# First feed-forward block: the down product by the seven-product scheme, the memory rows as a weight panel

## The reference, cut to what matters

```python
def swiglu(h, w_gate, w_up, w_down):              # 1024 -> 2816 -> 1024
    return (silu(h @ w_gate) * (h @ w_up)) @ w_down

shift1, scale1, gate1, shift2, scale2, gate2 = split(c_act @ ada_w[l] + ada_b[l], 6)
x = x + gate2[:, None, :] * swiglu(h, ...)        # layer 0
hk = modulate(rms_norm(x, kv_norm_g), k_shift, k_scale)   # then kv_a = hk @ w_kv_a
h  = modulate(rms_norm(x, norm1_g[1]), shift1, scale1)
mem_n = rms_norm_2(mem, mem_norm[l])              # memory rows, 256 x 1024
```

## Time and profile before

| | |
|---|---|
| median of 3 runs | 1117.94 us |
| profiled execution, its own time | 1117.15 us |
| its span | 1115.3 us |
| PE busy | 1052.3 us (94%) |
| DVE busy | 608.1 us (55%) |
| ACT busy | 294.0 us (26%) |
| DMA, mean over the span | 176 GB/s |

### The profile page before, as it was taken

The page is one execution under the profiler, slowest core; times in us unless marked ns, Lnnn a source line. Parts: engine busy times, 40 slices in busy tenths (PEclk is TensorE's granted clock), DMA queues, the critical chain, the costliest instruction groups (busy, mean ns, idle before and its releaser), DMA issues.

```text
span 1115.3 us, 21577 instructions
## 1 busy us (share of the span) xinstructions
PE 1052.3 (94%) x9373; PEld 909.2 (82%) x9373; DVE 608.1 (55%) x1180; ACT 294.0 (26%) x709; POOL 64.2 (6%) x84
## 2 busy tenths in 40 slices
PE   6879999999999999889999999999997799999997
PEld 4647888888888867678999999988887688898786
DVE  8996445444321727726766575334814561676632
ACT  6512510000000645623001000123323251202641
POOL 3010010110100100000000000000003100000000
PEclk9999999999999999999999999999998999999999
DMA  9995979999845334173654553443440003554220
GB/s 289 367 307 182 301 274 362 344 336 360 326 184 189 106 115 151 37 226 109 188 158 152 163 189 103 144 141 126 132 152 5 4 4 114 189 154 149 76 77 38
DMA packets 128744, 195.81 MB, mean 176 GB/s; under 512 B 4176, under 2 KB 114394, under 8 KB 122250
## 3 DMA queue, kind: packets, MB, share of 16 engines
q1 hardware_dynamic: 118218, 131.15, 37.0%
q0 software_dynamic: 10144, 62.92, 14.9%
q10 hardware_dynamic: 288, 0.36, 0.1%
HBM read 191.53 MB, written 1.05 MB: 173 GB/s over the span
## 4 chain that ended last, share of the span: by engine, by line
PE 82%; DVE 12%; ACT 3%; issue 2%; DMA 0%; SPq 0%; DVEq 0%; ACTq 0%
PE psum L761 45%; PE psum L1147 11%; PE psum L1233 7%; PE psum L1201 6%; DVE arena L1984 4%; PE psum L1774 3%; PE psum L1036 2%; PE psum L1739 1%; ACT arena L3085 1%; DVE sq L1984 1%; DVE arena L2154 1%; DVE arena L1990 1%; PE psum L1714 1%; DVE arena L2248 1%; ACT sq L3085 1%
## 5 line engine op out<-in xcount | busy, mean ns | idle before, releaser
L3085 ACT ACTIVATE arena<-psum 128x256 f32<-128x256 f32 (+6 forms) x229 | 100.6, 466 | 567.3 <-PE psum L761 341.7
L761 PE MATMUL psum<-hT,ring 128*128 128x256 f32 x944 | 211.6, 381 | 2.6 <-DVE hT L1990 1.4
L761 PEld LDWEIGHTS psum<-hT,ring 128*128 128x128 f32 x944 | 177.0, 190 | 30.0 <-issue 7.1
L761 PE MATMUL psum<-arena 64*64 64x64 f32 (+6 forms) x2252 | 91.4, 252 | 16.7 <-issue 11.4
L1984 DVE TENSOR_TENSOR arena<-arena 128x512 f32<-128x512 f32 (+8 forms) x145 | 97.5, 696 | 11.4 <-PE psum L1201 8.6
L761 PE MATMUL psum<-hT,arena 128*128 128x256 f32 (+2 forms) x664 | 94.7, 320 | 4.9 <-DVE hT L1984 4.9
L761 PEld LDWEIGHTS psum<-arena 64*64 64x64 f32 (+3 forms) x2252 | 71.8, 150 | 30.4 <-issue 26.9
L761 PEld LDWEIGHTS psum<-hT,arena 128*128 128x128 f32 (+2 forms) x664 | 82.6, 176 | 16.5 <-issue 6.7
L1984 DVE TENSOR_TENSOR arena<-psum,arena 128x128 f32<-128x128 f32 (+1 forms) x116 | 38.6, 353 | 74.3 <-PE psum L1147 41.1
L1984 DVE TENSOR_TENSOR arena<-arena,psum 128x512 f32<-128x512 f32 (+2 forms) x56 | 30.6, 570 | 72.8 <-ACT arena L3085 41.2
L1990 DVE SCALAR_TENSOR_TENSOR acc<-aring,c_act,acc 128x2048 f32<-128x2048 f32 (+1 forms) x21 | 41.9, 1994 | 37.9 <-DMA aring<-in_kv_ada_w 23.3
(11 more groups left out here) (322 smaller groups left out, 1568.4 us busy)
## 6 DMA issues: line engine op xcount, KB each, us to landing
aring<-in_ada_w POOLq DMA_DIRECT2D x36, 1024.0 KB, 8.4
ring<-in_a_w_in SPq DMA_DIRECT2D x14, 1024.0 KB, 5.4
arena<-in_ffn_w_gate SPq DMA_DIRECT2D x12, 1024.0 KB, 5.5
arena<-in_ffn_w_up SPq DMA_DIRECT2D x12, 1024.0 KB, 8.3
ring<-in_ffn_w_down SPq DMA_DIRECT2D x11, 1024.0 KB, 6.8
ring<-in_ffn_w_gate SPq DMA_DIRECT2D x10, 1024.0 KB, 8.7
ring<-in_ffn_w_up SPq DMA_DIRECT2D x10, 1024.0 KB, 9.5
ring<-in_ada_w POOLq DMA_DIRECT2D x8, 1024.0 KB, 14.4
```

The costliest lines, as they stand in the source:

```text
L761: return eng.matmul(dst, w, x, start=first, stop=last)
L3085: return eng.activation(dst, x, f, **k)
```

## The change

The hidden products of layer 0 stay as they are, chunk by chunk, but the down product now comes behind all of them and goes by the seven-product scheme, in the code that layer 1 uses. FAST names for each layer the j whose gate and up products are halved: none in layer 0. Further: the two sums of down panels 0 and 1 are made at j = 9; the ada panels are dealt out anew (22 of the 36 late ones up to j = 10, the other 14 between the steps of the down product); row blocks 3 to 6 move to later places; block 7 is summed between the two halves of kv_a; the sum of block 6 moves from sq to acc; the memory rows become an entry of the weight list (ring slot 0) behind the twelve down panels, and their transpose moves out of aring.

```diff
-        HALVED = (1,)
+        HALVED = (0, 1)
+        FAST = {0: (), 1: tuple(range(1, NDN))}
...
         swiglu_weights(0)
+        weights.append((a["mem_2"][0].rearrange("(b p) d -> p b d", p=P), (2, D), ("memT", 3)))
...
@@ TensorE
+            def whole_chunks(l, j, g, u):
+                for m in range(2):
+                    c = 2 * j + m
+                    eng.wait_ge(*next_bank(("gu", l, c)))
+                    ...
...
                     for q in range(DOWN_PANELS):
+                        beside_down(i, q)
...
-            def ada_beside(j):
-                if j in (2, 4, 6, 8):
-                    ada_rows(2 + j // 2)
-                if j in (3, 5, 7, 9):
-                    row_columns(2 + j // 2, row_late, "a")
-            swiglu(0, 0, ada_beside)
-            eng.wait_ge(done("mem_landed"), 16)
+            ROWS_AT, COLUMNS_AT = {3: 3, 7: 4, 9: 5}, {4: 3, 8: 4, 10: 5}
+            def ada_beside(j):
+                if j in ROWS_AT:
+                    ada_rows(ROWS_AT[j])
+                if j in COLUMNS_AT:
+                    row_columns(COLUMNS_AT[j], row_late, "a")
+            def ada_beside_down(i, q):
+                if (i, q) == (2, 0):
+                    ada_rows(6)
+                if (i, q) == (2, 2):
+                    row_columns(6, row_late, "a")
+            swiglu_of_halves(0, 0, ada_beside, ada_beside_down)
+            mem_nat, landed = panel()
+            eng.wait_ge(*landed)
...
-            ada_rows(7, "b")
             for b in range(2):
...
+                if b:
+                    ada_rows(7, "b")
@@ VectorE
                     if k == 0:
                         if blk > 4:
-                            eng.wait_ge(*filled_at(("row", blk - 2)))
+                            eng.wait_ge(*filled_at(("row", 3 if blk == 5 else blk - 1)))
...
+                    if j not in fast:
+                        for m in range(2):
+                            c = 2 * j + m
+                            combine_to(j + 1, m + 1)
+                            eng.wait_ge(*filled_at(("gu", l, c)))
+                            eng.wait_ge(done("silu_ready"), silus(l, c))
+                            tt(hid[:, c, :], hid[:, c, :], bank_of(("gu", l, c))[:, T:2 * T], ALU.mult)\
+                                .then_inc(*v.empties(("gu", l, c)))
+                            hid_done[0] = v.last
+                            beside(j, 1)
+                        combine_to(j + 1, 3)
+                        beside(j, 1)
+                        if j % 2 == 0 and j < NDN - 1:
+                            combine_hidden(l, [j - 2, j - 1])
+                        beside(j, 0)
+                        if j == NDN - 2:
+                            combine_down(l, 0)
+                            combine_down(l, 1)
+                        continue
...
-                combine_hidden(l, [NDN - 1])
+                combine_hidden(l, [8, 9, 10])
...
-                combine_down(l, 2)
-                combine_down(l, 3)
-                ahead = 4
+                ahead = 2
                 for i in range(KC // 2):
                     for d in range(ahead, min(3 * i + 6, DOWN_PANELS * KC // 2)):
                         combine_down(l, d)
+                        beside_down(i, d)
                     ahead = 3 * i + 6
+                    beside_down(i, None)
                     down_outputs(i)
...
-            def ada_beside(c):
-                for _ in range(2 if c < 14 else 1):
+            PANELS_BY = [2, 4, 6, 9, 11, 13, 16, 18, 20, 20, 22]
+            def ada_beside(j, n):
+                for _ in range(n):
+                    if ada_next[0] < EARLY + PANELS_BY[j]:
+                        ada_panel()
+                if n == 0 and j in (6, 10):
+                    ada_bias({6: 3, 10: 4}[j])
+            def ada_beside_down(i, d):
+                if d is not None:
                     ada_panel()
-                if c in (7, 11, 15, 19):
-                    ada_bias({7: 3, 11: 4, 15: 5, 19: 6}[c])
-            swiglu(0, ada_beside)
+                else:
+                    for _ in range((0, 0, 1, 3)[i]):
+                        ada_panel()
+                    if i in (1, 3):
+                        ada_bias(5 if i == 1 else 6)
+            swiglu_of_halves(0, 0, lambda i: None, ada_beside, ada_beside_down)
@@ ScalarE: the rows and columns are taken to match, and each block's first product is copied
+            def beside_down(pair):
+                if pair == 2:
+                    take_row(6, row_late)
+                if pair == 3:
+                    take_columns(6)
+                copy_down(0, pair)
+            squares(1, beside_down)
@@ GpSimd
-            eng.wait_ge(done("ada_used"), len(ada_source) - EARLY)
-            eng.dma_start(mem_nat, a["mem_2"][0].rearrange("(b p) d -> p b d", p=P)).then_inc(done("mem_landed"), 16)
```

More of the change, by code:

```diff
@@ L1133, in first_chunks, with swiglu_of_halves @@
                 last.then_inc(*fills(("gu", l, 1)))
-            def swiglu_of_halves(l, h_base):
+            def whole_chunks(l, j, g, u):
+                for m in range(2):
+                    c = 2 * j + m
+                    eng.wait_ge(*next_bank(("gu", l, c)))
+                    ps = bank_of(("gu", l, c)).rearrange("p (m t) -> p m t", t=T)
+                    for i, w in enumerate((g, u)):
+                        for k in range(KC):
+                            last = mm(ps[:, i, :], w[:, k, m * P:(m + 1) * P], hT3[:, k, :], k == 0, k == KC - 1)
+                    last.then_inc(*fills(("gu", l, c)))
+            def swiglu_of_halves(l, h_base, beside=lambda j: None, beside_down=lambda i, q: None):
                 g, landed = panel()
@@ L1217, in swiglu_of_halves @@
                         last.then_inc(*(fills(dn) if q == DOWN_PANELS - 1 else pe.signals("down_panel")))
[L1219 to L1249, removed]
-                        eng.wait_ge(*next_bank(("gu", l, c)))
-                        ps = bank_of(("gu", l, c)).rearrange("p (m t) -> p m t", t=T)
-                        for i, w in enumerate((g, u)):
-                            for k in range(KC):
-                                last = mm(ps[:, i, :], w[:, k, m * P:(m + 1) * P], hT3[:, k, :], k == 0, k == KC - 1)
-                        last.then_inc(*fills(("gu", l, c)))
-                    extra(j)
-                    if j:
-                        down(j - 1)
-                down(NDN - 1)
             def attend(at, steps):
@@ L2315, in combine_weights @@
                 g, u = slot(at), slot(at + 1)
-                s1, s2, s4 = [unit_sums(j)[:, x] for x in range(3)]
+                s1, s2, s4 = [unit_sums(l, j)[:, x] for x in range(3)]
                 if part == 1:
@@ L2382, in first_chunks, with swiglu_of_halves, combine_to @@
                 eng.wait_ge(*filled_at(("gu", l, 1)))
-                eng.wait_ge(done("silu_ready"), silu_base(l) + 2)
+                eng.wait_ge(done("silu_ready"), silus(l, 1))
                 tt(hid[:, 1, :], hid[:, 1, :], bank_of(("gu", l, 1))[:, T:2 * T], ALU.mult)\
                     .then_inc(*v.empties(("gu", l, 1)))
-            def swiglu_of_halves(l, h_base, behind):
+            def swiglu_of_halves(l, h_base, behind, beside=lambda j, n: None, beside_down=lambda i, d: None):
+                fast = FAST[l]
+                parts = [(j, part) for j in fast for part in range(1, 5)]
+                sent = [0]
+                def combine_to(j, part):
+                    while sent[0] < len(parts) and parts[sent[0]] <= (j, part):
+                        combine_weights(l, *parts[sent[0]])
+                        sent[0] += 1
@@ L2414, in swiglu_of_halves @@
                     two_ready = v.last
-                    if j < NDN - 1:
-                        combine_weights(l, j + 1, 3)
-                    else:
+                    if ahead:
+                        combine_to(j + 1, 3)
+                    if l and j == NDN - 1:
                         combine_down(l, 0)
@@ L2424, in swiglu_of_halves @@
                     tt(up[:, :, half_1], ps(p5), u3, ALU.add).then_inc(*v.signals("halves_read"))
-                    if j < NDN - 1:
-                        combine_weights(l, j + 1, 4)
-                    else:
+                    if ahead:
+                        combine_to(j + 1, 4)
+                    if l and j == NDN - 1:
                         combine_down(l, 1)
-                    if j % 2 == 0:
+                    beside(j, 1)
+                    if j % 2 == 0 and j < NDN - 1:
                         combine_hidden(l, [j - 2, j - 1])
@@ L3300, in swiglu_of_halves @@
                 for j in range(1, NDN):
+                    if j not in FAST[l]:
+                        for c in (2 * j, 2 * j + 1):
+                            eng.wait_ge(*filled_at(("gu", l, c)))
+                            act(hid[:, c, :], bank_of(("gu", l, c))[:, 0:T], ACT.Silu).then_inc(*s.signals("silu_ready"))
+                        beside(j)
```

(1 more changed line is left out.)

144 lines of the change are left out of this document (75 added, 69 removed).

## The result

The changed kernel's runs have a median of 1124.55 us (7 runs, 1122.7 to 1127.63) against 1119.52 us for the kernel before beside them (7 runs): ratio 1.0053, 95% interval 1.0039 to 1.0068. A second series gave 1.0039 (1.0026 to 1.0053). It is slower, by 4 to 6 us; "no change" was the forecast, and the time lies above its range. The profiled execution took 1123.88 us, its span 1122.1 us; PE was busy 1049.5 us (94%), DVE 649.8 us (58%), that is 42 us more than before.

The account below looks back on a forecast made before the run. The prediction took TensorE to bound the block. Its terms, -7.17 + 2.2 + 0.9 + 3.8 + 1.0 = +0.7 us on the profiled 1117.15, gave 1117.9, or 1118.7 us as median of runs; range 1112.5 to 1123.5.

Parts of the forecast that it names:

- products: Layer 0's down product: 308 products of 128 columns in 68.79 us in place of 75.96; -7.17 us.
- S: Down product, at the rows of block 6: PE waits for DVE to finish ada panel 28; +2.2 us.
- longer tail of the scheme: Behind the down product: x complete 1.9 us after PE's end, 1.07 before; +0.9 us.
- L: Tail: x late because DVE's last outputs stand behind ada panels waiting for loads; +3.8 us, 1.6 to 7.8 by load time.
- rows 7 between kv_a's halves: Row sums of block 7, moved from a gap ahead of kv_a onto the path between its halves; +1.0 us.
- clock from x to C: Slower TensorE clock from x complete to the second projection: nothing in the sum, priced only in rival (2).
- rival (2): The tail's idle lowers TensorE's clock into kv_a, from about 4 us idle; +2.3 us more, 1121.0 us; chance 0.17.
- upstream at nothing: Panels ahead of the down product, gate and up products, memory rows and weight loads: no added cost, 0 us.
- The aside that 6.15 us a load would give L = 3.2: Tail estimate using the Trainium skill's 6.15 us per 1 MB load for every load; not used in the sum.
- Rival (1): DVE delivers in time, so neither S nor L arises; -5.3 us, 1112.6 us; chance 0.25.
- Rival (3): Loads land in 8 us and more throughout, giving S = 4 and L = 8; +6.7 us, 1124.6 us; chance 0.13.

Follow-up runs that it names:

- e1_warm: The changed kernel with ten constant 128x256 products in PE's tail wait, ahead of the last squares' sums; 1116.25 us, ratio 0.9983 to the kernel before.
- m_late7: m_early with the rows of block 7 summed between kv_a's halves, not ahead of kv_a; 1113.67 us, ratio 0.9951.
- e2_no_last_three: The changed kernel with the last three late ada panels (34 to 36, block 7) neither loaded nor summed; 1120.45 us, ratio 1.0013.
- m_early: The changed kernel with 28 late panels by j = 10, rows 6 at (0, 2), rows 7 ahead of kv_a, no panel before last outputs; 1111.91 us, ratio 0.9938.
- before_late7: The kernel before the change, with only the rows of block 7 moved between kv_a's halves; 1119.49 us, ratio 1.0013.
- e3_rows_later: The changed kernel with the row sum of block 6 one down panel later, at (2, 1) not (2, 0); 1124.53 us, ratio 1.0055.
- e2_rows7_ahead: The changed kernel without the last three late ada panels and with the rows of block 7 summed ahead of kv_a; 1118.02 us, ratio 0.9990.
- e2_warm: e2_no_last_three with six constant 128x256 products ahead of the last squares' sums; 1115.55 us, ratio 0.9974.
- m_warm: m_early with six constant 128x256 products ahead of the last squares' sums; 1111.36 us, ratio 0.9932.

## Why the prediction was wrong

Its terms against what the traces measured, in us from F to C:

| term | predicted | after | second series |
|---|---|---|---|
| products | -7.17 | -7.19 | -7.19 |
| S, the wait at rows 6 (and its clock) | +2.2 | +2.80 | +4.08 |
| longer tail of the scheme | +0.9 | +0.86 | +0.86 |
| L, panels ahead of the last outputs | +3.8 | +4.66 | +2.30 |
| rows 7 between kv_a's halves | +1.0 | +1.19 | +1.19 |
| clock from x to C | 0 | +3.84 | +4.71 |
| sum | +0.7 | +6.16 | +5.95 |

Products: F to E without a wait (219.78 us in five kernels) against 226.97. S: F to E less 219.78. Longer tail and L: E to x is 1.07 before, 1.93 with no panel in front, and the rest L. Rows 7: K to C at full clock, 9.47 (e1_warm, m_late7), less 8.28. Clock: x to K beyond 5.26, and K to C beyond 9.47. That second part, 1.79 and 2.67 us, is just what kv_a's first half took beyond 4.12 us. The forecast missed by 5.5 us in the first trace, 3.84 of them clock, and by 5.3 in the second, 4.71 of them clock.

- **The step that failed is the clock, put at zero in the sum and kept to rival (2).** By its own numbers the forecast had an idle of L + 0.6 = 4.4 us and said that the clock decides from about 4; so the forecast case contained rival (2), and the sum had to hold its price. It was also mis-sized: 2.3 us taken from one stretch, where the tail shows 3.8 and 4.7. The slow clock lasted not for one block of matmuls but for a chain of short dependent ones and most of kv_a's first half (5.91 and 6.80 us for 4.12). e1_warm shows it: holding the clock alone takes the ratio from 1.0053 and 1.0039 to 0.9983, and the mean clock of the runs from 0.984 to 0.989.
- **The condition was wrong as well.** In e2_no_last_three and m_early the clock fell behind an idle of 0.82 us. The Trainium skill (TensorE: Matmul & The Clock Gate, section A second HAM failure mode: psum-queue depth-cycling) says of another kernel that frequent micro-idles between groups of matmuls make the gate swing. These traces agree in part: the clock fell at the 0.82 us, but m_late7 kept 1.00 with the same idle, and before_late7 lost it with none. What decides is open.
- **Products, longer tail, rows 7, upstream at nothing:** right to 0.1 us in the trace, rows 7 to 0.2. The memory rows and the weight panels made no wait, and gate and up chunks ran as before: F to E without the wait is 7.19 us shorter, which leaves nothing for them. Rows 7 cost 1.2 us in the traces; the 1.5 to 2.6 us of the runs can't be told from that.
- **S and L:** mechanism, place and order were as said (rows at 37.3 us into the product; behind them three waits of DVE for loads, of 2.80, 1.40 and 4.13 us; last add 6.59 us behind E). The S of 4.08 us in the second execution has more than 1 us of clock in it, as its wait was only 2.54 us. L swings with the landings, 4.66 and 2.30 us in two executions, within the spread given (1.6 to 7.8). The aside that 6.15 us a load would give L = 3.2 comes out as 3.4 by the same steps; nothing hangs on it. e3_rows_later shows that S and L are one chain on DVE: S taken away from PE alone returned in the tail.
- **Rival (1), DVE in time,** was what m_late7 reached term by term: -7.19 + 0.87 + 1.19 - 0.11 (x to K) make -5.24 in F to C, against the -5.3 of that rival, and -5.5 us by the runs. m_early has rows 7 ahead of kv_a and 0.94 of slow clock instead: -5.39, and -6.9 us by the runs. **Rival (3)** gave 1124.6 us, the measured time, by another mechanism: S and L weren't 4 and 8 but 2.80 and 4.66, and 4.08 and 2.30, and it has no clock in it. The agreement is chance.

The best version is m_early with or without two warm products: 1110.35 to 1111.91 us, 0.65% under the kernel before. The scheme brings what it promises once PE doesn't wait for the rows of block 6, no ada panel stands between the last product and x, and rows 7 stand ahead of kv_a. The middle one alone isn't enough: e2_no_last_three has 1.0013.

## What to carry to other kernels

When TensorE's work shrinks and another engine's row gets longer, look at the order of that engine at the end of the stage: whatever doesn't feed the next stage goes behind the outputs that do, or far ahead. Each new wait of PE has two prices, its length and the clock of the dependent chain behind it; put the second into the sum, from the whole chain, and not only into a rival. Where an idle can't be removed, products of constants in it can hold the clock: ten in an idle of 5.5 us gained 6 to 8 us in the runs. In a short idle they mustn't be longer than it; two in 0.82 us held the clock in the one traced execution, and the runs don't tell them from none.

## What the runs showed of the hardware

- The granted clock fell to 0.50 with no idle but 0.82 us (e2_no_last_three, m_early), and in before_late7 with PE busy 2.00 of 2 us, in a stretch of transposes and one-column products. A kernel with the same program up to there kept 1.00 (before, m_late7). So in these traces a tail of small matmuls had a clock that differed from execution to execution; I can't name what decides between the two. Averaged over a kernel's executions the granted clock still orders the kernels: 0.983 to 0.984 with long idle stretches in the tail (after, e3_rows_later), 0.986 where only the wait for the rows of block 6 is long (e2_no_last_three, e2_rows7_ahead), 0.989 where neither is (m_early), and 0.989 to 0.991 with constant products in the idle (e1_warm, e2_warm, m_warm).
- Behind a wait of 2.73 and of 2.54 us the rows took 1.07 us in one execution of the changed kernel and 1.94 in another.
- The stretch ahead of F, the same in all kernels, differed by 3.2 us between executions, about half of what separates the two spans (1115.3 and 1122.1 us).
